# Retention's heads and the last attention of an eight-layer block in another order

## The chip, the core and the metric

The kernel runs on one core of a Trainium2 chip. The metric is the device time of one execution in microseconds. TensorE does the matmuls and transposes, VectorE (DVE), ScalarE (ACT) and GpSimd (POOL) the elementwise work, and SyncE (SP) issues the weight transfers. Each engine works through its own queue in order and waits on semaphores.

## The reference

The input is 256 tokens of width 1024. Eight layers follow each other, all in fp32: stick-breaking attention (16 heads), a squared-ReLU MLP, retention (4 heads, chunks of 128), an MLP, gated linear attention, a convolutional FFN, NSA attention (here the "last attention"), and another FFN. Cut to the two that the change touches:

```python
# retention: q, k (4 heads x 256), v, g (4 heads x 512) = split(h @ w_in); q, k rotated
scores = einsum('bhnid,bhnjd->bhnij', qc, kc) * decay_in      # per 128-token chunk
o = inner + cross                                             # (B, 4, S, 512)
o = (o - mean(o)) * rsqrt(var(o) + eps)                       # per head
y = silu(g) * o;  out = y @ w_out                             # (2048 x 1024)

# NSA attention: 16 query heads in 4 groups over shared keys and values
k_cmp, v_cmp = gelu(blocks(kv) @ w1) @ w2                     # 15 overlapping blocks of 32
p_cmp = masked_softmax(q @ k_cmp * scale); o_cmp = p_cmp @ v_cmp
# with 256 tokens all 4 blocks of 64 are selected and the window of 512 covers all:
o_sel = masked_softmax(rope(q) @ k_sel) @ v_sel               # causal
o_win = masked_softmax(rope(q) @ k_win) @ v_win               # causal
out = (g0 * o_cmp + g1 * o_sel + g2 * o_win) @ w_o
```

## The kernel before

**Weights.** All large weights come as 212 pieces of 128 x 2048 fp32, numbered in the order of use (`ws`). SP streams half pieces into `ring`. ScalarE rounds each half to fp32r (`w_hi`, L1105), VectorE subtracts that for the rest (`w_lo`, L1500), and a product is three fp32r matmuls, hi*hi, hi*lo, lo*hi (`mm3`, L538 to L540). There are four slots for split pieces: `refill(g)` on ScalarE and VectorE splits piece g + 4 once TensorE has finished piece g. Where `refill` stands in an engine's queue is written out by hand. `transposed` makes features x tokens for one piece, `natural` tokens x features for two, `accumulate` and `close` add output pieces into banks 0 to 3.

**Retention.** After query and key pieces, seven pairs of pieces (c = 1 to 7) make values and gates. After pair 3 come the scores of the four heads. A head's output (`ret_out`, L771 and L774) comes after pairs 5, 6, 7 and then once more. `ret_norm` (VectorE) takes its statistics (L1782, L1783) and multiplies by the gate (L1785), GpSimd raises the variance to -0.5 (L416), `ret_scale` (ScalarE) multiplies (L1285). When all four heads are on the way, TensorE runs `keep_clock(3)` (L503), matmuls whose results nobody reads, then turns the eight pairs of 128 columns (`transpose_pair`, L652) between six output pieces G_RET+24 to G_RET+29, and closes with G_RET+30 and G_RET+31.

**The last attention.** Pieces from G_NSA on: two for values, four for compression input and keys (G_NSA+2 to +5), four for queries (+6 to +9), four for the compression's first layer (+10 to +13), four for the output (+14 to +17). Around them on TensorE: the input is turned a second time under another gain (`turn_over("7b", t)`), a small product makes the gates, `ns_swap` multiplies by a permutation for the rotation. VectorE adds positions to the blocks (L1954, 32 instructions), scales, and adds the rope products (L1981, L1988). The keys stand twice in `ns_kd`, each copy with zeros in the other 64 partitions (memset by GpSimd).

Then 16 steps `it`, first the eight pairs of heads of branch 0, then those of branch 1. A step is: `ns_qk_` (L1028, L1029), 128-row products for two heads into banks 4 and 5; `ns_scores` (VectorE): mask added (L2065), maximum (L2070); `ns_exp` (ScalarE, L1439), four exponentials with their sums; `ns_coef` (VectorE): reciprocal times gate (L2078, L2081); a product on GpSimd (L487); `ns_t_`, six transposes (L1036) into banks 6 and 7; `ns_copy` (ScalarE, L1444); `ns_pv_` (L1050, L1051) into banks 0 to 3, where all sixteen heads stay open. Scores run two steps ahead. The compressed branch (`ns_cmp_...`) is fitted in, `keep_clock(4)` stands before the steps and `keep_clock(3)` after them. Only then come the splits of the outputs (L1468, L1554) and the output pieces.

## Time and profile before

| | |
|---|---|
| time, median of 3 runs | 1426.49 us (1425.15 to 1429.76) |
| profiled execution | 1426.23 us, span 1424.5 us |
| busy: TensorE, VectorE, ScalarE, GpSimd | 1366.0, 922.6, 724.5, 122.6 us |
| mean granted TensorE clock | 0.986 |
| weights moved | 231 MB at 162 GB/s |

Times in the profile count from the start of the span. A matmul's record has its pipeline's end in it, so records of neighbours overlap, and the distance of starts is the cost of one. An fp32 matmul is two records. The granted clock is a share of 2.4 GHz; 0.5 would be 1.2 GHz throughout.

### The profile page before, as it was taken

Reading aid. Unit: us, or ns where it says so; the run is one execution under the profiler, and the core shown is the slowest. Engines: PE = TensorE matmul, PEld = TensorE weight load, DVE = VectorE, ACT = ScalarE, POOL = GpSimd, SP = SyncE. Lnnn points to the kernel's source line nnn. Section 1 sums busy time; section 2 is a strip of 40 time slices with the busy share of each in tenths; the row PEclk is TensorE's granted clock in tenths of the full one; section 3 lists DMA queues with packets and bytes.
Section 4 is the critical chain, followed back from the end, with each engine's and each line's share of the span. In section 5 each row is a group of like instructions: output and inputs, shape, how many; then the busy total and the mean of one; then the engine's idle time right before and its main releaser. Section 6 shows DMA issues by size and latency. Waiting matters only on the chain.

```text
span 1424.5 us, 22775 instructions
## 1 busy us (share of the span) xinstructions
PE 1366.0 (96%) x8754; PEld 1218.0 (86%) x8754; DVE 922.6 (65%) x1353; ACT 724.5 (51%) x1139; POOL 122.6 (9%) x123
## 2 busy tenths in 40 slices
PE   8999999999999899999999999999999778999997
PEld 7887999889987679998888789999889556899996
DVE  5666655557645456555577569777768765697775
ACT  5555444445344345444473456555474455565552
POOL 0101000003400000000002300000004133000000
PEclk9999999999999999999999999999999999999999
DMA  6435655555644346555554345555463101355551
GB/s 237 156 124 197 209 182 197 183 173 189 194 161 165 102 150 212 182 198 183 172 163 148 118 150 184 192 185 187 168 221 120 45 31 59 126 191 186 189 192 64
DMA packets 63309, 231.06 MB, mean 162 GB/s; under 512 B 7024, under 2 KB 7280, under 8 KB 63216
## 3 DMA queue, kind: packets, MB, share of 16 engines
q1 hardware_dynamic: 61632, 224.42, 46.9%
q10 hardware_dynamic: 1584, 5.31, 1.1%
q8 instruction: 69, 1.13, 0.3%
q14 instruction: 24, 0.20, 0.0%
HBM read 228.66 MB, written 1.05 MB: 161 GB/s over the span
## 4 chain that ended last, share of the span: by engine, by line
PE 85%; DVE 6%; ACT 3%; DMA 2%; issue 2%; POOL 1%; SPq 0%; POOLq 0%; DVEq 0%; ACTq 0%
PE ps L538 26%; PE ps L540 26%; PE ps L539 26%; DMA ring<-ws 2%; DVE w_lo L1500 2%; ACT w_hi L1105 1%; PE ps L852 1%; POOL arena L487 1%; PE ps L515 1%; PE ps L1029 1%; ACT x_hi L1121 1%; PE ps L1036 1%; DVE arena L2065 0%; PE ps L1028 0%; DVE arena L2070 0%
## 5 line engine op out<-in xcount | busy, mean ns | idle before, releaser
L1500 DVE TENSOR_TENSOR w_lo<-ring,w_hi 128x1024 fp32r<-128x1024 f32 x424 | 514.2, 1253 | 188.6 <-ACT w_hi L1105 188.2
L1105 ACT ACTIVATE w_hi<-ring 128x1024 fp32r<-128x1024 f32 x424 | 429.5, 1054 | 283.6 <-PE ps L540 216.6
L538 PE MATMUL ps<-x_hi,w_hi 128*128 128x256 f32 x1664 | 473.8, 285 | 2.5 <-DVE x_lo L1516 2.5
L539 PE MATMUL ps<-x_lo,w_hi 128*128 128x256 f32 x1664 | 471.8, 284 | 0.0
L540 PE MATMUL ps<-x_hi,w_lo 128*128 128x256 f32 x1664 | 471.7, 283 | 0.0
L538 PEld LDWEIGHTS ps<-x_hi,w_hi 128*128 128x128 f32 x1664 | 320.3, 192 | 5.8 <-issue 4.7
L539 PEld LDWEIGHTS ps<-x_lo,w_hi 128*128 128x128 f32 x1664 | 320.4, 193 | 1.0
L540 PEld LDWEIGHTS ps<-x_hi,w_lo 128*128 128x128 f32 x1664 | 320.2, 192 | 0.0
L538 PE MATMUL ps<-w_hi,y_hi 128*128 128x512 f32 (+1 forms) x624 | 244.2, 391 | 8.4 <-issue 8.0
L539 PE MATMUL ps<-w_lo,y_hi 128*128 128x512 f32 (+1 forms) x624 | 240.4, 385 | 0.0
L540 PE MATMUL ps<-w_hi,y_lo 128*128 128x512 f32 (+1 forms) x624 | 240.0, 385 | 0.0
L538 PEld LDWEIGHTS ps<-w_hi,y_hi 128*128 128x128 f32 x624 | 117.7, 189 | 33.2 <-issue 10.2
L540 PEld LDWEIGHTS ps<-w_hi,y_lo 128*128 128x128 f32 x624 | 117.5, 188 | 23.9
L539 PEld LDWEIGHTS ps<-w_lo,y_hi 128*128 128x128 f32 x624 | 117.8, 189 | 22.3 <-issue 1.0
L538 PE MATMUL ps<-w_hi,x_hi 128*128 128x512 f32 x240 | 97.7, 407 | 4.2 <-DVE w_lo L1500 4.1
L540 PE MATMUL ps<-w_hi,x_lo 128*128 128x512 f32 x240 | 94.5, 394 | 0.0
L539 PE MATMUL ps<-w_lo,x_hi 128*128 128x512 f32 x240 | 94.2, 392 | 0.0
L392 POOL TENSOR_TENSOR stat<-stat,power 128x1 f32<-128x1 f32 x20 | 11.5, 583 | 917.1 <-DVE stat L1493 917.1
L1549 DVE SCALAR_TENSOR_TENSOR arena<-ps,arena 128x512 f32<-128x512 f32 x64 | 44.2, 690 | 70.7 <-PE ps L540 70.7
L1187 ACT ACTIVATE arena<-arena,sm 128x256 f32<-128x256 f32 x88 | 48.2, 596 | 60.2 <-DVE arena L1549 60.2
L1121 ACT ACTIVATE x_hi<-ps,sm 128x128 fp32r<-128x128 f32 x144 | 39.1, 382 | 65.8 <-PE ps L515 65.8
L1155 ACT ACTIVATE arena<-ps 128x512 f32<-128x512 f32 x32 | 19.2, 598 | 92.8 <-PE ps L540 92.8
(205 smaller groups left out, 1238.9 us busy)
## 6 DMA issues: line engine op xcount, KB each, us to landing
ring<-ws SPq DMA_DIRECT2D x424, 512.0 KB, 4.7
tab<-tables ACTq DMA_DIRECT2D x3, 550.0 KB, 4.2
rowg<-rows ACTq DMA_DIRECT2D x3, 512.0 KB, 6.1
h<-x SPq DMA_DIRECT2D x2, 512.0 KB, 4.4
out<-arena SPq DMA_DIRECT2D x2, 512.0 KB, 2.6
arena<-decay ACTq DMA_DIRECT2D x1, 768.0 KB, 9.3
sm<-small ACTq DMA_DIRECT2D x1, 642.0 KB, 5.8
arena<-narrow ACTq DMA_DIRECT2D x1, 296.0 KB, 2.7
```

The source lines that it names most:

```text
L487: r = gp.tensor_tensor(v, v, f, ALU.mult)
L515: r = nc.tensor.transpose(ps[:, 4 + k // 2, t * T + (k % 2) * P:t * T + (k % 2 + 1) * P], h[:, t, k * P:(k + 1) * P], ident)
L538: mm(o, lh, rh, start=start, stop=False, skip_group_check=True)
L539: mm(o, lh, rl, start=False, stop=False, skip_group_check=True)
L540: return mm(o, ll, rh, start=False, stop=stop, skip_group_check=True)
L852: r = mm(o, keys, q, start=True, stop=True, skip_group_check=True)
L1105: A(w_hi[:, g % RING, c:c + HALF], ring[:, q % RAW, :], ACT.Copy).then_inc(hi_ready, 1)
L1121: r = A(x_hi[:, k, t * P:(t + 1) * P], ps[:, 4 + b, t * T + (k % 2) * P:t * T + (k % 2 + 1) * P], ACT.Copy, scale=gain(n, k))
L1155: A(relu[:, u % 2, :], ps[:, bank(u), :], ACT.Relu).then_inc(freed, 1)
L1187: r = A(conv[:, u % 2, e, :], conv_in[:, u % 2, e, :], ACT.Identity, scale=par(u, 4 + e), bias=par(u, 6 + e))
L1500: V.tensor_tensor(w_lo[:, g % RING, v], ring[:, q % RAW, :], w_hi[:, g % RING, v].bitcast(F32), ALU.subtract).then_inc(lo_ready, 1)
L1549: return V.scalar_tensor_tensor(dst, src.rearrange("p (a t) -> p a t", t=T), by, sc.unsqueeze(1).broadcast_to([P, 2, T]), ALU.mult, ALU.mult)
```

## The change

**Retention.** The outputs of heads 0 to 3 are computed inside the gate pairs 4 to 7, in banks given by `rt_o`, and heads 0 and 1 are turned inside pairs 6 and 7, heads 2 and 3 inside output pieces G_RET+25 and G_RET+27 (banks `rt_t`). `ret_norm` moves in front of the refills of its pair. `keep_clock(3)` goes.

**The last attention.** The arena is laid out anew. The second turning stands between pieces G_NSA+4 and +5 and goes to `y_hi`, `y_lo`. The compression's four pieces come after the first query piece, as G_NSA+7 to +10, and the other three query pieces are +11 to +13; the host's order of pieces follows. The steps run by pairs: `it // 2` is the pair of heads, `it % 2` the branch. Steps 0 to 3 lie between the compression pieces and in query piece +11, steps 4 to 6 between the other query pieces; from step 4 on scores are three steps ahead. Scores use 64 rows for each head: each key stands in both halves of the partitions (VectorE writes one half, ScalarE copies the other, `ns_kd_other`), with no zeros. `ns_scores` becomes four `tensor_tensor_reduce`, which add the mask, negate and take the minimum. The copies of turned scores are split: bank 6 by ScalarE, bank 7 by VectorE. A pair's sum over three branches is made in 128 columns of banks 6 and 7 (`ns_o`), then split by `ns_hi` (ScalarE) and `ns_lo` (VectorE) into `x_hi`, `x_lo`; the compressed branch is in two halves (`c`). With banks 0 to 3 free, output pieces G_NSA+14 and +15 are added in eight parts inside the steps (`ns_fill`, six matmuls each); +16 and +17 close as before. The 32 block additions become two instructions on GpSimd, whose rotation products of queries move to steps 3 to 5. Both `keep_clock` go.

The diff, cut to its core and moved left (retention and attention on TensorE, then ScalarE, then VectorE):

```diff
+rt_o = ((0, 1), (2, 3), (0, 1), (6, 7))
+rt_t = ((2, 3), (0, 1), (4, 5), (6, 7))
...
+    pe.wait_ge(*((ret_decayed, 4), (ret_decayed, 4), (ret_o_free, 2), (ret_vg, 14))[hd])
+    pe.wait_ge(ret_vg, 8)
...
+def ret_turn(hd):
+    pe.wait_ge(ret_y, 2 * hd + 2)
+    pe.wait_ge(*((ret_o_free, 4), (ret_o_free, 6), (ret_vg, 16), (ret_o_free, 8))[hd])
+    for j in range(2):
+        transpose_pair(rt_t[hd][j], rt_g, 2 * hd + j).then_inc(ret_transposed, 1)
...
+    then = {4: {(1, 0): lambda: ret_out(0)},
+            5: {(0, 1): lambda: ret_out(1)},
+            6: {(0, 1): lambda: ret_out(2), (1, 0): lambda: ret_turn(0)},
+            7: {(0, 1): lambda: ret_out(3), (1, 0): lambda: ret_turn(1)}}.get(c)
...
-ret_out(3)
-pe.wait_ge(ret_vg, 16)
-keep_clock(3)
...
+pe.wait_ge(ret_yT_lo, 4)
+accumulate(G_RET + 24, (0, 1), True)
+accumulate(G_RET + 25, (2, 3), False, mid=lambda: ret_turn(2))
+accumulate(G_RET + 26, (4, 5), False)
+accumulate(G_RET + 27, (6, 7), False, mid=lambda: ret_turn(3))
+pe.wait_ge(ret_yT_lo, 6)
+accumulate(G_RET + 28, (0, 1), False)
+accumulate(G_RET + 29, (2, 3), False)
+pe.wait_ge(ret_yT_lo, 8)
+close([(G_RET + 30, (4, 5)), (G_RET + 31, (6, 7))], 3)
...
+def ns_qk(it):
+    pr, br = it // 2, it % 2
+    if it < 2:
+        pe.wait_ge(nsa_kd_other, it + 1)
+        pe.wait_ge(nsa_sin, 2)
+    if it >= 5:
+        pe.wait_ge(nsa_cmp_scores_copied, 1 if it < 6 else 2)
+    if it >= 6:
+        pe.wait_ge(nsa_cmp_pT_copied, 1 if it < 8 else 2)
+    pe.wait_ge(nsa_roped, pr // 2 + 1)
+    if it:
+        pe.wait_ge(nsa_max, it)
     for i in range(2):
-        kd, q = ns_kd[i][:, br, pr // 2, :], ns_qr[:, pr, :]
-        mm(ps[:, 4 + i, 0:P], q[:, 0:P], kd[:, 0:P], start=True, stop=True)
-        r = mm(ps[:, 4 + i, P:384], q[:, P:T], kd, start=True, stop=True)
+        v = slice(64 * i, 64 * i + 64)
+        kd, q = ns_kd[v, br, pr // 2, :], ns_qr[v, pr, :]
+        mm(ps[:, 4 + i, 0:P], q[:, 0:P], kd[:, 0:P], start=True, stop=True, skip_group_check=True)
+        r = mm(ps[:, 4 + i, P:384], q[:, P:T], kd, start=False, stop=True, skip_group_check=True)
...
+def ns_t(it):
     pe.wait_ge(nsa_p, it + 1)
+    if it:
+        pe.wait_ge(nsa_pT_copied, it)
+        pe.wait_ge(nsa_pT_copied2, it)
+    if it >= 4:
+        pe.wait_ge(nsa_oT_lo, max(it // 2, 2))
     for i in range(2):
...
+def ns_pv(pr):
+    pe.wait_ge(nsa_pT_copied, max(2 * pr + 2, 4))
+    pe.wait_ge(nsa_pT_copied2, max(2 * pr + 2, 4))
+    pe.wait_ge(nsa_cmp_pT_copied, pr // 4 + 1)
+    if pr:
+        pe.wait_ge(nsa_oT_lo, pr)
+    for t in range(TT):
+        mm(ns_o[:, t, :], ns_vbd[:, pr // 4, 2 * (pr % 4):2 * (pr % 4) + 2, :], ns_cp[:, 2 * (pr // 4) + t, :],
+           start=True, stop=False, skip_group_check=True)
+    for br in range(2):
+        for i in range(2):
+            v = ns_v[:, :, br * 256 + (pr // 2) * 64:br * 256 + (pr // 2) * 64 + 64]
+            p_ = ns_p[(2 * pr + br) % 4][:, i, :]
+            for t in range(TT):
+                o = ps[64 * i:64 * i + 64, 6 + t, 384:512]
+                r = mm(o, v[:, 0, :], p_[:, t * P:(t + 1) * P], start=False, stop=False, skip_group_check=True)
+            r = mm(o, v[:, 1, :], p_[:, T:384], start=False, stop=br == 1, skip_group_check=True)
...
+def ns_fill():
+    n = filled[0]
+    filled[0] += 1
+    i, k, t = n // 4, n // 2 % 2, n % 2
+    if n == 0:
+        pe.wait_ge(nsa_roped, 4)
+    if t == 0:
+        pe.wait_ge(nsa_oT_lo, n // 2 + 1)
+        split(G_NSA + 14 + i, k)
+    r = add(G_NSA + 14 + i, (2 * i, 2 * i + 1), t, k, i == 0, False, (x_hi, x_lo))
...
+ns_qk(0)
+ns_first(0, 1)
+ns_qk(1)
+ns_first(1, 0)
+ns_t(0)
+ns_qk(2)
+ns_first(1, 1)
+ns_t(1)
+ns_qk(3)
 ns_hidden_t()
-keep_clock(4)
-for it in range(16):
-keep_clock(3)
...
+pe.wait_ge(nsa_gate_in, 1)
+transposed(G_NSA + 11, 1, src=mixed, mid=lambda: ns_t(2))
+ns_t(3)
+ns_swap(3)
+transposed(G_NSA + 12, 0, src=mixed, mid=lambda: (ns_cmp_kv(), ns_qk(4)))
+ns_cmp_qk(0)
+ns_qk(5)
+ns_swap(4)
+pe.wait_ge(nsa_roped, 2)
+transposed(G_NSA + 13, 1, src=mixed, mid=lambda: ns_cmp_t(0))
+ns_pv(0)
+ns_cmp_qk(1)
+ns_swap(5)
+ns_qk(6)
+ns_pv(1)
+for it in range(4, 16):
+    ns_t(it)
+    if it == 5:
+        ns_cmp_t(1)
+        ns_fill()
+    if it + 3 < 16:
+        ns_qk(it + 3)
+    if it in (6, 7, 10, 11, 14):
+        ns_fill()
+    if it % 2:
+        ns_pv(it // 2)
+        if it in (9, 13):
+            ns_fill()
+pe.wait_ge(nsa_oT_lo, 8)
+close([(G_NSA + 16, (4, 5)), (G_NSA + 17, (6, 7))], 8, src=(x_hi, x_lo))
...
+    if c >= 5:
+        ret_scale(c - 5)
     refill(G_RET + 9 + 2 * c)
-    if c >= 6:
-        ret_scale(c - 6)
-ret_scale(2)
+refill(G_RET + 24)
+ret_turned(2)
+refill(G_RET + 25)
 ret_scale(3)
-for g in range(10):
-    if g < 8:
...
+refill(G_RET + 26)
+refill(G_RET + 27)
+ret_turned(3)
+refill(G_RET + 28)
+refill(G_RET + 29)
...
+ns_exp(1)
+refill(G_NSA + 9)
+ns_copy(0)
+ns_exp(2)
+refill(G_NSA + 10)
+ns_inner_(1)
+ns_copy(1)
+ns_exp(3)
 ns_gelu_square()
-for it in range(16):
-    if it:
...
+ns_copy(2)
+ns_gelu_tanh()
+refill(G_NSA + 11)
+ns_copy(3)
+ns_cmp_keys()
+ns_exp(4)
+refill(G_NSA + 12)
+ns_cmp_exp(0)
+ns_exp(5)
+ns_cmp_copy(0)
+refill(G_NSA + 13)
+ns_hi(0)
+ns_cmp_exp(1)
+ns_hi(1)
+for it in range(4, 16):
+    ns_copy(it)
     if it == 5:
-        act.wait_ge(nsa_cmp_shifted, 1)
-        A(ns_cs[:, :, :, :], ns_cs[:, :, :, :], ACT.Exp).then_inc(nsa_cmp_exp, 1)
...
+        ns_cmp_copy(1)
+    if it + 2 < 16:
+        ns_exp(it + 2)
+    if it in (10, 15):
+        refill(G_NSA + (14 if it == 10 else 15))
+    if it % 2:
+        ns_hi(it // 2)
...
 def ns_scores(it):
     dve.wait_ge(nsa_scores, it + 1)
     if it >= 3:
         dve.wait_ge(nsa_pT, it - 2)
-    s = ns_s[:, it % 3, :, :]
-    V.tensor_tensor(s, ps[:, 4:6, 0:384],
-                    tab[:, C_CAUSAL:C_CAUSAL + 384].unsqueeze(1).broadcast_to([P, 2, 384]), ALU.add)\
-     .then_inc(nsa_masked, 1)
-    dve.wait_ge(nsa_masked, it + 1)
-    for t in range(2):
-        r = V.tensor_reduce(ns_m[:, it % 2, :, t], s[:, :, P * t:P * t + P * (t + 1)], AX.X, ALU.max,
-                            negate=True)
+    if it >= 2:
+        dve.wait_ge(nsa_exp, it - 1)
+    for i in range(2):
+        for t in range(TT):
+            v = slice(P * t, P * t + P * (t + 1))
+            r = V.tensor_tensor_reduce(ns_s[it % 3][:, i, v], ps[:, 4 + i, v],
+                                       tab[:, C_CAUSAL + v.start:C_CAUSAL + v.stop], -1.0, 3.0e38,
+                                       ALU.add, ALU.min, ns_m[:, it % 2, i, t:t + 1])
     r.then_inc(nsa_max, 1)
...
 ns_scores(0)
+V.memset(ns_kc[:, :, :], 0.0)
 ns_coef(0)
 ns_scores(1)
+refill(G_NSA + 8)
+ns_coef(1)
+ns_copy(0)
+ns_scores(2)
+refill(G_NSA + 9)
+ns_coef(2)
+link(V.memset(ns_h[:, 2:4, :, :], 0.0))
+ns_copy(1)
+ns_scores(3)
 ns_gelu_inner()
-for it in range(16):
+ns_coef(3)
+refill(G_NSA + 10)
+ns_copy(2)
+ns_queries(1)
+ns_gelu()
+ns_copy(3)
+ns_rope(1)
+refill(G_NSA + 11)
+ns_cmp_values()
+ns_scores(4)
+ns_queries(2)
+ns_cmp_scores(0)
+ns_coef(4)
+ns_scores(5)
+ns_cmp_p(0)
+ns_rope(2)
+ns_coef(5)
+refill(G_NSA + 12)
+ns_queries(3)
+ns_lo(0)
+ns_cmp_scores(1)
+ns_rope(3)
+ns_scores(6)
+refill(G_NSA + 13)
+ns_lo(1)
+for it in range(4, 16):
+    ns_copy(it)
+    if it + 3 < 16:
+        ns_scores(it + 3)
+    if it == 4:
+        ns_cmp_p(1)
     if it + 2 < 16:
-        ns_scores(it + 2)
-    if it == 3:
...
+        ns_coef(it + 2)
+    if it % 2:
+        ns_lo(it // 2)
+    if it == 11:
+        refill(G_NSA + 14)
+refill(G_NSA + 15)
```

## Rows read from the trace of the kernel before

**Rows 1.** Page, part 1: engine, busy us, share of the span, instructions.
```profile
PE 1366.0 (96%) x8754; PEld 1218.0 (86%) x8754; DVE 922.6 (65%) x1353; ACT 724.5 (51%) x1139; POOL 122.6 (9%) x123
```

**Rows 2.** Waits of TensorE, 380 to 500 us: total, times, longest.
```profile
PE ps L538 <- issue: 5.6, 1, 5.6
```

**Rows 3.** Waits of TensorE, 1050 to 1220 us.
```profile
PE ps L1036 <- POOL arena L487: 7.1, 7, 2.5
PE ps L1028 <- DVE arena L1988: 6.0, 1, 6.0
```

**Rows 4.** Windows: length, busy us and instructions per engine, granted clock, DMA.
```profile
465.35:480.01 14.66, 9.03 (x30) 4.47 (x30) 9.45 (x18) 8.35 (x13) 1.39 (x2) 0.88 0.31 110
480.01:487.28 7.27, 7.27 (x26) 5.83 (x27) 1.09 (x2) 0.15 (x1) 0.00 (x0) 0.77 0.01 2
1039.67:1063.00 23.33, 23.27 (x195) 23.07 (x193) 13.71 (x14) 15.57 (x21) 0.00 (x0) 1.00 0.74 254
1063.00:1118.77 55.77, 46.77 (x342) 42.37 (x343) 47.67 (x88) 23.66 (x37) 16.03 (x8) 0.93 0.35 120
1118.77:1203.40 84.63, 69.08 (x435) 50.25 (x435) 54.90 (x114) 50.19 (x161) 31.97 (x32) 0.94 0.12 38
1203.40:1214.30 10.90, 10.90 (x48) 9.04 (x49) 2.36 (x2) 2.01 (x2) 0.00 (x0) 1.00 0.14 37
```

**Rows 5.** Chain, 430 to 500 us: start, us, engine and line.
```profile
438.37 1.72 PE ps L771 x4
440.09 0.86 PE ps L774 x2
...
487.28 0.44 PE ps L652 x4
```

**Rows 6.** Timeline of TensorE in stick-breaking attention, from 43 us.
```profile
43.10 0.50 PE L670 MATMUL ps<-arena 64*128 64x128 f32 x4
43.42 0.61 PE L672 MATMUL ps<-arena 64*128 64x256 f32 x4
43.96 0.38 PE L538 MATMUL ps<-x_hi,w_hi 128*128 128x256 f32 x1
```

**Rows 7.** Timeline of TensorE in the last attention, from 1151 us.
```profile
1150.81 0.87 PE L1036 MATMUL ps<-sm,arena 128*128 128x128 f32 x6
1151.52 0.39 PE L1028 MATMUL ps<-arena 128*128 128x128 f32 x2
...
1152.17 0.38 PE L1028 MATMUL ps<-arena 128*128 128x128 f32 x2
```

**Rows 8.** Groups by form, 1118 to 1203 us: count, busy, mean ns, idle before.
```profile
L1439 ACT ACTIVATE arena<-arena 128x256 f32<-128x256 f32 x32 | 15.9, 496 | 0.0
L2065 DVE TENSOR_TENSOR arena<-ps,tab 128x768 f32<-128x768 f32 x16 | 15.3, 954 | 14.8 <-PE ps L1029 14.8
...
L1439 ACT ACTIVATE arena<-arena 128x128 f32<-128x128 f32 x32 | 12.5, 392 | 6.5 <-DVE arena L2070 6.5
...
L1439 ACT ACTIVATION_READ_ACCUMULATOR arena<-arena 128x1 f32 x64 | 12.1, 190 | 0.0
...
L2070 DVE TENSOR_REDUCE arena<-arena 128x2 f32<-128x512 f32 x16 | 10.8, 676 | 0.0
...
L2070 DVE TENSOR_REDUCE arena<-arena 128x2 f32<-128x256 f32 x16 | 6.7, 420 | 0.6
L503 PE MATMUL ps<-sm 128*128 128x512 f32 x14 | 6.5, 607 | 0.0
```

**Rows 9.** Groups of VectorE, whole span.
```profile
L1712 DVE TENSOR_TENSOR_SCAN arena<-arena,tab 128x384 f32<-128x384 f32 x16 | 14.6, 956 | 17.7 <-ACT arena L1232 17.7
```

**Rows 10.** Timeline of GpSimd, 1163 to 1171 us.
```profile
1164.72 3.50 POOL L487 TENSOR_TENSOR arena<-arena 128x256 f32<-128x256 f32 x2 [3.85 <-DVE arena L2081]
1169.60 1.61 POOL L487 TENSOR_TENSOR arena<-arena 128x256 f32<-128x256 f32 x2 [1.38 <-DVE arena L2081]
```

**Rows 11.** Windows of 10 us.
```profile
1180.00:1190.00 10.00, 7.84 (x62) 6.07 (x59) 9.09 (x17) 5.71 (x21) 5.12 (x4) 1.00 0.41 133
```

More of the change, by code:

```diff
@@ new lines, in ns_swap, with ns_first @@
+                b, src = (4 + i, ns_k[:, i, :, :]) if i < 2 else (i % 2, ns_q[:, 2 * (i - 2):2 * (i - 2) + 2, :])
+                mm(ps[:, b, :], swap, src, start=True, stop=True).then_inc(nsa_swapped, 1)
+            def ns_first(i, e):
+                g = G_NSA + 7 + 2 * i + e
+                s = g % RING
+                pe.wait_ge(nsa_blocks, i + 1)
+                for l in range(8):
+                    if l % 4 == 0:
+                        split(g, l // 4)
+                    w, x = l * 256, (16 * i + 8 * e + l) * 60
+                    r = mm3(ps[:, 2 + i, 0:256], ns_xhf[:, x:x + P], ns_xlf[:, x:x + P],
+                            w_hi[:, s, w:w + 256], w_lo[:, s, w:w + 256], e + l == 0, e * l == 7)
+                r.then_inc(done, 1)
@@ new lines, in ns_kd_other @@
+            def ns_kd_other(br):
+                act.wait_ge(nsa_kd, br + 1)
+                for o in range(2):
+                    r = A(ns_kd[64 - 64 * o:128 - 64 * o, br, o:o + 3:2, :], ns_kd[64 * o:64 * o + 64, br, o:o + 3:2, :],
+                          ACT.Copy)
+                r.then_inc(nsa_kd_other, 1)
+            refill(G_NSA + 2)
+            ns_raw_(0)
+            refill(G_NSA + 3)
+            ns_raw_(1)
+            tiles("7b", 0, y_hi, 0)
+            refill(G_NSA + 4)
+            tiles("7b", 1, y_hi, 0)
@@ new lines, in _ @@
+            refill(G_NSA + 5)
+            for i in range(2):
+                act.wait_ge(nsa_blocks_f32, i + 1)
+                A(ns_xh[:, i, :, :], ns_x[:, i, :, :], ACT.Copy).then_inc(nsa_blocks_hi, 1)
+            for br in range(2):
+                ns_kd_other(br)
+            refill(G_NSA + 6)
+            act.wait_ge(nsa_gate_scaled, 1)
+            A(ns_gt[0:48, :], ns_gt[0:48, :], ACT.Sigmoid).then_inc(nsa_gates_transposed, 1)
+            refill(G_NSA + 7)
+            act.wait_ge(nsa_gates_turned, 1)
@@ L1960, in _, with ns_queries @@
[L1960 to L1966 removed]
+            def ns_queries(u):
+                dve.wait_ge(done, G_NSA + (7 if u == 0 else 11 + u))
+                scaled(ns_q[:, 2 * u:2 * u + 2, :], ps[:, u % 2, :], scale, 0.125).then_inc(nsa_q_in, 1)
@@ new lines, in _ @@
+            ns_unit(0)
+            refill(G_NSA + 2)
+            ns_unit(1)
+            refill(G_NSA + 3)
+            tiles("7b", 0, (y_hi, y_lo), 0)
+            ns_unit(2)
+            refill(G_NSA + 4)
+            tiles("7b", 1, (y_hi, y_lo), 0)
+            ns_unit(3)
+            refill(G_NSA + 5)
+            for i in range(2):
+                dve.wait_ge(nsa_blocks_hi, i + 1)
+                V.tensor_tensor(ns_xl[:, i, :, :], ns_x[:, i, :, :], ns_xh[:, i, :, :].bitcast(F32), ALU.subtract)\
+                 .then_inc(nsa_blocks, 1)
@@ new lines, in _ @@
+            for br in range(2):
+                ns_sin(br)
+                dve.wait_ge(nsa_sin, br + 1)
+                dve.wait_ge(nsa_cos_product, br + 1)
+                for o in range(2):
+                    v = slice(64 * o, 64 * o + 64)
+                    r = V.tensor_tensor(ns_kd[v, br, o:o + 3:2, :], ns_t1[v, br, :, :], ns_t2[br][v, :, :], ALU.add)
+                r.then_inc(nsa_kd, 1)
+            ns_queries(0)
+            refill(G_NSA + 6)
+            dve.wait_ge(nsa_small_proj, 1)
```

557 lines of the change are left out of this document (218 added, 339 removed).

## The prediction

> **What bounds the kernel now.** I read the busy shares first: TensorE holds 96% of the span [rows 1], so a change pays where it removes TensorE idle time, dead work, or half-clock time, and nowhere else. Then the waits of TensorE around the two stages that the diff touches. In retention there is one wait, 5.6 us [rows 2]. In the last attention (NSA) there are many; the largest sums are for GpSimd's coefficient product (L487) and the rope sums of VectorE (L1988) [rows 3]. The windows say how much there is in all and at which clock [rows 4]. Then the chain, for what one instruction group costs on TensorE [rows 5], and the groups by form for the queues behind it [rows 8].
>
> **Retention.** From the end of the last gate piece (465.35) to the first output piece (480.01) pass 14.66 us [rows 4]. Of these, work that stays: ret_out of heads 2 and 3, each 1.72 + 0.86 = 2.58, so 5.16, and three pairs of transposes at 0.44 = 1.32 [rows 5]. The other 8.2 us are keep_clock and the wait, and both go. The wait is a chain over other engines: ret_norm on VectorE, the power on GpSimd, ret_scale on ScalarE, then the copies of the turned pairs. Then the first output piece runs at a low clock: 7.27 us, granted clock 0.77, that is a stretch at 1.2 GHz (the lower of the two levels) after the 5.6 us wait; a piece at full clock takes 10.90 / 2 = 5.45 [rows 4]. Another 1.8. Sum: 10.0.
>
> Is something late in its place? I followed each new wait. A gate pair is now 10.9 + 2.58 (+ 0.88 for two turned pairs), 13.5 to 14.4 us. ret_norm(hd) stands ahead of the refill in VectorE's queue; it takes about 3.2 us (four operations of 512 elements at 0.68 as the reduction of that size [rows 8], three small ones) from the gate's evacuation, and the refill behind it fills a slot four pieces (some 22 us) ahead, so TensorE doesn't see that. ret_turn(0) asks for a head normalised a whole pair earlier. The tightest is ret_turn(1): it needs ret_norm(2) off banks 0 and 1, which stands behind refill(G_RET+21); I find it done about 1.4 us early. ret_turned(2) on ScalarE waits for the piece that used its y tile (done of G_RET+25) with refill(25) behind it: again 20 us of cover. If one of these misses, it costs 1 to 2 us: the stage gives 8 to 10.3.
>
> **NSA, what goes.** I take the stage from 1039.67 (its third piece) to 1214.30, where the last two output pieces start: 174.6 us. In it TensorE is idle 55.77 - 46.77 = 9.0 and 84.63 - 69.08 = 15.55, so 24.55 [rows 4]. keep_clock takes 6.5 [rows 8]. The scores of a step cost 2 x 0.65 = 1.3 us with full 128-row keys, half of them zeros (1151.52 to 1152.17 is one head) [rows 7]; the new form, 64 rows for each of two heads, is in stick-breaking attention: 43.10 to 43.96 = 0.86, since the two heads overlap [rows 6]. 16 x 0.43 = 6.9 saved. Stretches at 1.2 GHz inside the two windows (clock 0.93 and 0.94) [rows 4] cost about 4 beyond the idle time: my estimate, as idle time is in that mean too. Transposes, pieces and swaps keep their columns. Floor: 174.6 - 24.55 - 6.5 - 6.9 - 4 = 132.6 us.
>
> **NSA, what the new order waits for.** The chain of a step is: scores, mask and maximum on VectorE, four exponentials on ScalarE (2 x 0.39 + 2 x 0.50 = 1.8), coefficient on VectorE (two operations of four elements, 0.4 with the hand-over), product on GpSimd (1.61 for its two instructions alone, 3.50 where VectorE's weight refill runs beside it [rows 10]), transposes 0.87 [rows 7]. Three steps of lead on TensorE are 10 us, more than this chain. So GpSimd, 7.1 us of waits before, drops out; what is left is queues in order.
>
> The new instruction, a fused tensor_tensor_reduce, isn't in this trace. Before, a step has 0.95 + 0.42 + 0.68 = 2.05 on VectorE [rows 8]. Now four instructions of 128, 256, 128, 256 elements. Low end: the rate of those rows (256 elements in 0.42, 512 in 0.68: 0.16 fixed and 1 ns an element), so 0.29 and 0.42, 1.4 a step. High end: the scan, 384 elements in 0.956, so 2.07 ns an element [rows 9]: with it 2.2, and with four reads of the accumulator at ScalarE's 0.19 for such a read [rows 8], up to 3.0. I take 1.8: the full rate, since its nearest row is the mask addition (PSUM plus table), and 0.1 for each minimum written out. The page "VectorE: DVE Perf Modes" of the Trainium skill (Two Vector instructions with no wait between them) says that an op that also writes its accumulator is two instructions; that speaks against the fusion, eight entries where there were three. ScalarE's rows of that kind agree, VectorE has none here.
>
> The thirty-two block additions leave VectorE for two instructions of 960 elements on GpSimd: 2.0 each by the 768 elements in 1.61, 4.4 by the 3.50 [rows 10]. Both are due only at the first compression piece, some 20 us after their inputs; cover enough, cost nothing. If it were gone: up to 4. The page "SBUF — State Buffer" of the Trainium skill (Who interferes with whom) has this as a lock: a VectorE op with two SBUF inputs and a GpSimd op that reads SBUF exclude one another. The two rows of GpSimd agree (1.61 and 3.50); it would give the same sum, only place the stretched copies beside the refills.
>
> Walked in order with these prices, TensorE waits at:
> 1. gates and first rope (VectorE has the keys, q scaling, a refill and the gate product before them): 1.3.
> 2. ns_hidden_t: ScalarE has the exponentials of step 2 (1.8), a refill (2.0 [rows 4]) and ns_inner_(1) (0.4) to do, 4.2; TensorE has at that time 0.7 of compression and scores 3 (0.86): 2.6.
> 3. ns_t(3), for VectorE's copy behind refill(G_NSA+10), and cmp_qk(0): 1.2.
> 4. ns_t(4), which wants the low half of pair 1. On VectorE stand before it, from the last swap on, the last rope (1.5), scores 6 (1.8), refill(G_NSA+13) (2.4 [rows 4]) and ns_lo(1) (0.4), 6.7 with hand-overs; TensorE has scores 6 and value product 1, 3.1: 3.6.
> 5. ns_cmp_t(1): in the first loop turn VectorE does scores 7 (1.8, once they are there) and the compressed probabilities (1.6: two operations of 256 elements, three small); TensorE has ns_t(5), 0.87: 2.7.
> 6. Each pair's end: transposes of the next pair share banks 6 and 7 with the sums, so they wait for ns_hi and ns_lo (256 elements each, 0.4 and a hand-over each), 1.0; covered by ns_fill only after steps 9 and 13. With the refill in step 11 and the last pair: 9.0 in all.
>
> Sum 20.4, I take 21. The waits 2, 4 and 5 are long enough to bring the clock down, as the long ones before did [rows 4], and there is no keep_clock now: three times 1.5 to 2, so 5. NSA: 174.6 - 132.6 - 21 - 5 = 16 less. The output pieces G_NSA+14 and 15 are inside the loop as ns_fill (8 x 6 matmuls of 512 columns, 10.9 us); they are in both sums. Weights: no DMA is added, SP's queue keeps its length and streams pieces four ahead; the compression pieces only change places with three query pieces. What is moved to ScalarE (four key copies of half the partitions, eight ns_hi in place of four copies) is in the walk.
>
> **Sum.** The profiled execution took 1426.2 (span 1424.5), the median of the runs is 1426.5. 10 + 16 = 26 less: **1400** us. By the bounds: some twelve of the sixteen steps are on the path. With 1.4 for the fused step (12 x 0.4) and no clock loss the stage gives 10 more: 1390. With 2.7 a step 12 x 0.9 = 11 come back: 1411.
>
> **Rivals.**
> - *The waits almost vanish.* VectorE is busy 47.7 + 54.9 us of 140.4 [rows 4] and the order leaves it other work at each wait. For: stick-breaking attention and GLA interleave likewise. Against: six waits above each have a named instruction in front. If 8 of the 26 us (waits and clock) remain: 1426 - 10 - 34 = 1382 to 1390.
> - *VectorE becomes the bound.* The fused instruction runs at the scan's rate or its reads are dear (2.7 to 3.0 us a step). For: two operations and a sum in one. Against: the mask addition, its nearest row, runs at 1 ns an element. 12 steps x 0.9 to 1.2, so 11 to 14 back: 1411 to 1414.
> - *Nothing in NSA.* The fills and query pieces only move work, and every gap is closed by a new one of its size: 1416.
> - *Slower: the half clock.* keep_clock stood where TensorE's work was thin. If the steps of the loop stay at 1.2 GHz after the wait at ns_t(4), the loop's TensorE work of 42 us takes as much again (12 transposes 10.4, 9 scores 7.7, fills 10.9, and 6 value products of fourteen 128-column matmuls: 0.215 each by the 512 columns in 0.86 [rows 5], twelve of them overlapping by a third as the scores do, 2.15): 26 gained, 42 less the 12 of waits in the loop lost, so 1430. It decides from 26 us of uncovered half-clock work on. For: [rows 4] show 0.93 and 0.94 over both halves. Against: from 1180 on TensorE is busy only 7.84 of 10 us, in short waits, and the clock stays at 1.00 [rows 11].
>
> **Chances.** Forecast (1392 to 1408) 0.57; waits vanish 0.18; VectorE the bound 0.16; nothing in NSA 0.05; slower 0.04. The range takes in the first two and most of the third: 1386 to 1412. This kernel's runs can tell 0.3%, 4 us. Faster 0.95, same 0.01, slower 0.04.
>
> **What the profile after would show.** Retention: no TensorE wait over 1 us between the gates and the close, clock 1.00 there, no L503-like matmuls in it; else the first part is wrong. NSA: the fused instruction at 0.27 to 0.42 us for 128 and 256 elements with a short read behind; scores of a step 0.86 on TensorE; no wait on GpSimd's product; waits at ns_hidden_t, ns_t(4), ns_cmp_t(1), and about 1 us before the transposes of even steps. The prediction falls if the fused form costs over 0.7 us for 256 elements, or if the low clock lasts beyond each of the long waits.

## The result, and the profile after

The changed kernel takes 1393.1 us (median of 4 runs, 1391.5 to 1396.5) beside 1427.4 us for the kernel before, run with it: ratio 0.976, 95% interval 0.974 to 0.978. That is 34 us less; 26 were forecast, with a range of 1386 to 1412. The profiled execution took 1391.5 us (span 1389.8). It is the fastest of the four, and the one with the highest mean granted clock: 0.995, where the others have 0.992, 0.990 and 0.989 in the order of their times.

The page's busy shares, which answer to [rows 1]:

```profile
PE 1343.2 (97%) x8814; PEld 1204.1 (87%) x8814; DVE 909.6 (65%) x1423; ACT 722.0 (52%) x1149; POOL 122.1 (9%) x123
```

TensorE was the bound and still is. It did 23 us less of work in more instructions, and its share rose by one point. VectorE has 70 more instructions and 13 us less work.

Windows of the kernel after (length, busy us and instructions per engine, granted clock, DMA share, GB/s): first retention, from the scores to the turn of the second row tile; then the last attention (NSA), from its third piece to the close of the last two output pieces; then three parts of it: up to the transposes of step 4, the 12 us from there, and the whole loop from there. They answer to [rows 4].

```profile
408.51:512.03 103.52, 103.52 (x461) 82.31 (x460) 55.84 (x72) 46.28 (x57) 6.43 (x4) 1.00 0.48 163
1028.40:1179.55 151.15, 133.70 (x1086) 115.78 (x1084) 105.82 (x288) 90.66 (x232) 43.78 (x40) 0.99 0.34 112
1063.00:1125.00 62.00, 53.85 (x442) 47.21 (x442) 50.56 (x132) 36.67 (x88) 18.49 (x16) 1.00 0.37 121
1125.00:1137.00 12.00, 9.14 (x64) 6.53 (x64) 5.72 (x28) 5.12 (x20) 3.22 (x4) 0.86 0.23 80
1125.00:1178.61 53.61, 45.24 (x362) 34.92 (x362) 25.94 (x116) 29.11 (x102) 16.10 (x20) 0.97 0.12 39
```

The first row is retention without a gap: TensorE is busy for all of 103.52 us at clock 1.00. Between the same two instructions the kernel before took 113.59 (411.35 to 524.94), so 10.1 less. The second row is NSA: 151.15 against 174.63, so 23.5 less. Of the 151.15 us TensorE is busy for 133.70 and idle for 17.45 (before: 150.02 and 24.6). By distances of starts the 23.5 us are 7.1 of waits, 6.4 of keep_clock and some 11 of scores (25.6 to 14.7, low clock in both); everything else together costs about 1 us more than before. The only low clock of the stage is in the 12 us of the fourth row, 0.86. The remaining difference of the two profiled executions lies in code that is the same in both: 2.8 us less ahead of retention and 1.6 more between the stages. Both are differences between executions, not between the kernels. The first: in the second run of the changed kernel (below) retention ends 1.8 us later than in this profile, without any edit. The second is one stretch at the lower clock that begins at 799.7, behind a wait of 2.3 us: of the fourteen profiles of this case eight have it and take 516.0 us between the stages, the other six, the kernel before among them, 514.3 to 514.4, with the same waits.

The waits of TensorE in NSA (total us, times, longest), which answer to [rows 3]:

```profile
PE ps L1027 <- DVE x_lo L2158: 5.5, 4, 2.4
PE ps L959 <- ACT arena L1450: 2.1, 1, 2.1
PE ps L994 <- DVE arena L2126: 2.0, 1, 2.0
PE ps L1039 <- ACT arena L1492: 1.6, 2, 0.9
PE ps L939 <- DVE arena L1639: 1.4, 1, 1.4
PE ps L1027 <- DVE arena L2166: 1.1, 1, 1.1
PE ps L544 <- DVE x_lo L2158: 0.9, 1, 0.9
PE ps L1078 <- ACT arena L1521: 0.9, 1, 0.9
...
PE ps L1014 <- DVE arena L2064: 0.6, 1, 0.6
...
PE ps L1027 <- POOL arena L491: 0.2, 1, 0.2
```

The first row is step transposes (L1027) waiting for the low half of a pair (L2158): once 2.4 before step 4, then three times 1.02, before steps 6, 8 and 12. GpSimd's product, 7.1 us in [rows 3], is down to 0.2, and the 6.0 for the rope sums to 0.6 (L2064). No single wait is longer than 2.4.

Groups of VectorE's instructions in the steps, 1080 to 1186 us, by form:

```profile
L2138 DVE CUSTOM_DVE_ANT_0 arena<-ps,tab 128x256 f32<-128x256 f32 x28 | 11.7, 419 | 0.0
...
L2138 DVE CUSTOM_DVE_ANT_0 arena<-ps,tab 128x128 f32<-128x128 f32 x28 | 8.0, 287 | 5.2 <-PE ps L1015 5.1
...
L2138 DVE DVE_READ_ACCUMULATOR2_ANT arena<- 128x1 f32 x56 | 4.6, 83 | 0.0
```

These are the two sizes of the fused instruction and its read, the price that the trace of before could not give. The timeline of VectorE below, up to the longest wait, shows them in line:

```profile
1121.06 0.28 DVE L2138 CUSTOM_DVE_ANT_0 arena<-ps,tab 128x128 f32<-128x128 f32 x1
1121.27 0.08 DVE L2138 DVE_READ_ACCUMULATOR2_ANT arena<- 128x1 f32 x1
1121.27 0.42 DVE L2138 CUSTOM_DVE_ANT_0 arena<-ps,tab 128x256 f32<-128x256 f32 x1
...
1122.16 2.35 DVE L1590 TENSOR_TENSOR w_lo<-ring,w_hi 128x1024 fp32r<-128x1024 f32 x2
1124.44 0.42 DVE L2158 TENSOR_TENSOR x_lo<-ps,x_hi 128x256 fp32r<-128x256 f32 x1
1125.89 0.56 DVE L2166 COPY arena<-ps 128x384 f32<-128x384 f32 x1 [1.03 <-PE ps L1027]
```

A read starts at the same time as the next fused instruction and so costs nothing; a step of four takes 1.19 us (1121.06 to 1122.24). Behind it stands the weight refill, 2.35 us, and only then the low half, at whose end (1124.86) TensorE's transposes start (1125.00).

### The profile page after: what moved, and what is told of

It is laid out like the page before. It is cut to its first block, busy times and chain, and to the rows that moved or that the text cites. A ratio compares the mean times of both kernels' runs of the same rounds, so it can differ in the third digit from the quotient of the medians.

```text
span 1389.8 us, 23087 instructions
## 1 busy us (share of the span) xinstructions
PE 1343.2 (97%) x8814; PEld 1204.1 (87%) x8814; DVE 909.6 (65%) x1423; ACT 722.0 (52%) x1149; POOL 122.1 (9%) x123
## 4 chain that ended last, share of the span: by engine, by line
PE 87%; DVE 5%; ACT 3%; DMA 2%; issue 2%; POOL 1%; SPq 0%; POOLq 0%; DVEq 0%; ACTq 0%
PE ps L544 26%; PE ps L546 26%; PE ps L545 26%; DMA ring<-ws 2%; DVE w_lo L1590 2%; ACT w_hi L1148 1%; PE ps L854 1%; PE ps L521 1%; ACT x_hi L1164 1%; PE ps L1047 1%; PE ps L1027 1%; PE ps L777 0%; DVE arena L2138 0%; ACT arena L1141 0%; PE ps L1015 0%
## 5 line engine op out<-in xcount | busy, mean ns | idle before, releaser
L544 PE MATMUL ps<-x_hi,w_hi 128*128 128x256 f32 x1600 | 454.5, 284 | 2.5 <-DVE x_lo L1606 2.5
L545 PE MATMUL ps<-x_lo,w_hi 128*128 128x256 f32 x1600 | 452.7, 283 | 0.0
L546 PE MATMUL ps<-x_hi,w_lo 128*128 128x256 f32 x1600 | 452.7, 283 | 0.0
L544 PE MATMUL ps<-w_hi,y_hi 128*128 128x512 f32 x560 | 220.3, 393 | 2.3 <-issue 2.3
L545 PE MATMUL ps<-w_lo,y_hi 128*128 128x512 f32 x560 | 219.0, 391 | 0.0
L546 PE MATMUL ps<-w_hi,y_lo 128*128 128x512 f32 x560 | 218.7, 391 | 0.0
L544 PE MATMUL ps<-w_hi,x_hi 128*128 128x512 f32 (+1 forms) x304 | 121.9, 401 | 5.8 <-DVE w_lo L1590 4.8
L546 PE MATMUL ps<-w_hi,x_lo 128*128 128x512 f32 (+1 forms) x304 | 116.3, 382 | 0.0
L545 PE MATMUL ps<-w_lo,x_hi 128*128 128x512 f32 (+1 forms) x304 | 115.9, 381 | 0.0
L544 PEld LDWEIGHTS ps<-w_hi,x_hi 128*128 128x128 f32 x304 | 57.4, 189 | 21.9 <-DVE w_lo L1590 5.5
```

Of the source, the lines that this page charges most:

```text
L544: mm(o, lh, rh, start=start, stop=False, skip_group_check=True)
L545: mm(o, lh, rl, start=False, stop=False, skip_group_check=True)
L546: return mm(o, ll, rh, start=False, stop=stop, skip_group_check=True)
```

## Experiments

The experiments were run in four groups on three chips: the second run of the changed kernel (1394.4 us) stands beside the late refill, the moved parts and both; retention alone, the fused instruction, the 128-row scores and the shorter lead form the second group; the blocks, the output parts and the clock the third; the last kernel the fourth. In each group the kernel before was run too, with medians of 1427.4, 1426.5, 1428.3 and 1427.1 us, so two groups compare within 1 to 2 us. "More" and "less" below are against the changed kernel's 1393.1 and 1394.4, and a ratio is always against the kernel before of the same group. "The stretch" is that from the first rope swap of NSA (L939) to the start of the close, read from each kernel's timeline of TensorE: 123.4 us in the profile after, 124.3 in that second run of the same kernel.

**The changed kernel again.** No edit.

> The changed kernel once more, on the chip and beside the runs of the next three kernels. Both theories expect 1393.1 us within 1 us; it gives the mark for differences of 2 to 5 us.

Measured: 1394.4 us (1393.8 to 1395.0, 5 runs), ratio 0.977 (0.975 to 0.979). A difference of 1 us between two groups of runs means nothing here. Its profile has nearly the same waits as the profile after, but two stretches at the lower clock in NSA instead of one.

**Retention alone.** The kernel before, with only the part of the diff that concerns retention (rt_o and rt_t, ret_out and ret_turn inside the gate pieces, the new order on ScalarE and VectorE).

> The kernel before with the retention part of the change alone. Theory: the 10.0 us of that part are on TensorE's path and independent of the last attention: 1427.4 - 10.0 = 1417.4, ratio 0.993. Rival: the gain is given back in the stages behind (weights or queues that come late there): within 2 us of the kernel before.

Measured: 1416.6 us (1415.0 to 1418.4), before beside it 1426.5; ratio 0.993 (0.991 to 0.995), 9.9 us less. From scores to the second turn pass 103.7 us (410.31 to 513.99), with no wait of TensorE from 380 to 500. The theory holds and nothing is given back behind it; so some 24 of the 34 us are NSA's.

**The fused instruction taken apart.** ScalarE's exponentials then take the scores with their own sign (scale=-1.0 goes).

```diff
-                for i in range(2):
-                    for t in range(TT):
-                        v = slice(P * t, P * t + P * (t + 1))
-                        r = V.tensor_tensor_reduce(ns_s[it % 3][:, i, v], ps[:, 4 + i, v], ...)
+                V.tensor_tensor(s, ps[:, 4:6, 0:384], <causal table>, ALU.add).then_inc(nsa_masked, 1)
+                dve.wait_ge(nsa_masked, it + 1)
+                for t in range(2):
+                    r = V.tensor_reduce(ns_m[:, it % 2, :, t], s[:, :, P * t:P * t + P * (t + 1)], AX.X, ALU.max,
+                                        negate=True)
```

> The changed kernel with the fused instruction taken apart again, as it was before: a mask addition for both heads, then two negated maxima (2.05 us a step by the rows of before, where the fused form takes 1.19). Theory of the prediction: some twelve of the sixteen steps lie on the path, 12 x 0.86 = 10 us more, 1403. Rival: three steps of lead cover VectorE (busy only half of the loop), so that just the places where its queue is already late lose: 0 to 3 us more, 1393 to 1396.

Measured: 1403.1 us (1401.5 to 1404.2), ratio 0.983 (0.982 to 0.985): 9 to 10 more. The size is that of "twelve steps on the path", but the trace doesn't show twelve delayed steps. Its waits and one window (TensorE):

```profile
PE ps L1027 <- DVE x_lo L2160: 6.3, 4, 3.2
PE ps L959 <- ACT arena L1450: 2.8, 1, 2.8
...
PE ps L1014 <- DVE arena L2141: 1.8, 2, 1.4
PE ps L1039 <- issue: 1.7, 1, 1.7
PE ps L1027 <- POOL arena L491: 1.3, 1, 1.3
```
```profile
1129.83:1142.00 12.17, 10.03 (x52) 7.17 (x54) 5.87 (x14) 4.86 (x19) 1.61 (x2) 0.60 0.24 79
```

The stretch is 131.3 us, 7 to 8 more. About 5 of them are waits, grown in five places by 0.7 to 1.1 each; the rest is the clock, which after the 3.19 us wait stays near its lower level (1.2 GHz) for most of 12 us (0.60 granted, where the same place in the kernel after has 0.86). So VectorE's time counts where its queue is already late, and the longest wait is paid a second time in the clock.

**Scores over all 128 rows.**

```diff
-                    kd, q = ns_kd[v, br, pr // 2, :], ns_qr[v, pr, :]
+                    kd, q = ns_kd[:, br, pr // 2, :], ns_qr[:, pr, :]
```

> The changed kernel with scores over all 128 rows for each head, so 1.3 us a step instead of 0.86 on TensorE; the scores are then sums over both heads of a pair, which leaves the result wrong and the amount of all other work as it is. Theory: TensorE bounds the stage, 16 x 0.43 = 6.9 us, less what lies in its waits: 5 to 7 more, 1398 to 1400. Rival: the other engines' chains set the pace, the longer scores fill waits: 0 to 2 more.

Measured: 1399.8 us (1397.7 to 1400.1), ratio 0.981 (0.979 to 0.983): 5 to 7 more, as the theory has it. The profiled execution (the fastest of the four) shows less: its stretch is 126.7, 2.4 to 3.3 more. There the longer scores filled waits (that for the hidden units, L959, fell from 2.1 to 0.3). What the other runs lost beyond that was not profiled, so between 2 and 7 us is what can be said for the row tiles.

**Scores two steps ahead.** In the loop, on TensorE, ScalarE and VectorE (ns_scores and ns_coef, moved like the lines below); GpSimd's order needs no edit. In step 5 the scores also come ahead of ns_cmp_t(1).

```diff
-                if it + 3 < 16:
-                    ns_qk(it + 3)
+                if 5 <= it < 14:
+                    ns_qk(it + 2)
...
-                if it + 2 < 16:
-                    ns_exp(it + 2)
+                if 5 <= it < 15:
+                    ns_exp(it + 1)
```

> The changed kernel with scores two steps ahead instead of three in the loop (steps 5 to 15), on all four engines. Theory: the third step of lead is what took GpSimd's product off the path; with two the chain of 5.8 to 7.7 us stands against 5.6 to 7.4 us of TensorE work, and waits of up to 2 us ended by the product (L491) come back in nine steps: 3 to 10 us more, 1396 to 1403. Rival: pairs and fills alone do it, the lead is slack: 0 to 1 more.

Measured: 1410.5 us (1409.3 to 1413.2), ratio 0.989 (0.987 to 0.991): 16 to 17 more, beyond the theory's 10. Waits:

```profile
PE ps L1027 <- POOL arena L491: 14.9, 6, 4.0
PE ps L1027 <- DVE x_lo L2158: 5.5, 4, 2.4
```

The named wait is the right one, but it comes in five steps, not nine, and is not "up to 2 us": it stands before the transposes of every odd step from 7 on, 2.0 at steps 7 and 11 and 3.0 to 4.0 at 9, 13 and 15 (and 0.4 before step 3). The product itself takes its 1.61 us in both kernels; it starts later, since the coefficient (and all before it) starts later. The loop's clock is 0.91 from 1138 to the end, where the kernel after has 1.00 (1137 to 1178.6). Of all parts of the change that were undone here, this one is worth most.

**The block additions back on VectorE.**

```diff
+                for l in range(16):
+                    o = ns_x[:, i, l, :].rearrange("p (a n) -> p a n", n=15)
+                    ...
+                    r = V.tensor_scalar(o, ns_raw[:, i, :, 2 * l:2 * l + 16 * 14 + 1:16], pe_, None, ALU.add)
```

> The changed kernel with the additions of the compression blocks back on VectorE, thirty-two instructions of 60 elements at 345 ns with their hand-over (6.7 us busy in the kernel before), and the two on GpSimd left out. Theory: VectorE's queue is what gates, rope and query pieces wait for there, so that 2 to 5 of these microseconds show, 1395 to 1398. Rival: the fold into the lead of the query piece covers them all: within 1 us of the changed kernel.

Measured: 1401.9 us (1401.6 to 1403.7), ratio 0.982 (0.981 to 0.984): 7.5 to 9 more, outside both. A wait and a window:

```profile
PE ps L932 <- DVE arena L1632: 7.8, 1, 7.8
```
```profile
1058.00:1074.00 16.00, 8.35 (x60) 7.18 (x59) 15.84 (x43) 3.87 (x5) 3.24 (x1) 0.82 0.22 76
```

The third rope swap (L932) waits 7.8 us for the scaled query (L1632), where the changed kernel waits 1.4 (0.7 in its second profile): VectorE is busy for 15.84 of 16.00 us, with the 32 additions (7.0 us) in front of the keys' rope and the query. Before the change four query pieces lay between the additions and the work that reads them; now the first swap of the queries comes right behind its piece. GpSimd does the same work in two instructions of 2.34 us each, and nothing waits for them. The part's worth is not the engine time saved but the place in the queue.

**The output parts out of the loop.** All eight ns_fill after it, with both refills of those slots.

> The changed kernel with the two output pieces (eight parts, 10.9 us of TensorE work) taken out of the loop and done after it, all else equal. Theory: the loop's chains, not TensorE's work, end its waits only at pair ends; by the waits that the parts stand beside, 1 to 4 us open up: 1394 to 1397. Rival one: the parts were wholly in idle time, all 10.9 us show: 1404. Rival two: they covered nothing: 1393.

Measured: 1399.5 us (1398.6 to 1402.4), ratio 0.981 (0.980 to 0.983): 5 to 6 more, between the theory's 1 to 4 and the rival's 10.9. The loop from the transposes of step 4 to the last value product (windows):

```profile
1128.48:1176.49 48.01, 36.03 (x315) 27.68 (x315) 23.76 (x114) 25.20 (x98) 16.09 (x20) 0.93 0.07 22
```

48.0 us without the parts, 53.6 with them (above): of 10.9 us of work 5.6 cost time in the loop, and 5.3 lie in waits or in what the lower clock takes (0.93 here, 0.97 above). Those 5.3 are what the parts inside the loop save, and the 5 to 6 more measured agree.

**A late refill, parts moved, and both.**

```diff
             ns_scores(6)
-            refill(G_NSA + 13)
             ns_lo(1)
             for it in range(4, 16):
                 ns_copy(it)
+                if it == 5:
+                    refill(G_NSA + 13)
```
```diff
                 if it == 5:
-                    ns_cmp_t(1)
                     ns_fill()
+                    ns_cmp_t(1)
...
-                if it in (6, 7, 10, 11, 14):
+                if it in (6, 10, 14):
                     ns_fill()
                 if it % 2:
                     ns_pv(it // 2)
-                    if it in (9, 13):
+                    if it in (7, 9, 11, 13):
                         ns_fill()
```

> VectorE's weight refill of piece G_NSA+13 goes from before the low half of pair 1 to after the copy of step 5. Theory: the wait before the transposes of step 4 (2.39 us, ended by that low half) is the refill's 2.4 us and goes; the stretch at the lower clock right behind it goes as well: 2.4 to 4.1 us less than the changed kernel, 1389.0 to 1390.7. Rival: another queue is as late there (ScalarE's copy of the high half), or the refill only moves the delay to the low half of pair 2: within 0.7 us of the changed kernel.

> The pieces of output work inside the loop change places: in step 5 ahead of the turned compressed probabilities, in steps 7 and 11 behind the value product instead of ahead. Theory: they then lie over the waits before those turns (2.0 us) and before the transposes of steps 8 and 12 (1.02 us each): 1.4 + 1.0 + 1.0 = 3.4 us less, 1389.7. Rival: where they stood they covered waits of the same size (the value products wait for ScalarE's copies), which open now: within 0.7 us of the changed kernel.

> The two edits before this one together. Theory: the waits are apart and their gains add: 5.8 to 7.5 us less than the changed kernel, 1385.6 to 1387.3. Rival: both shorten one chain, so that together they give no more than the larger alone: 1389 to 1391.

Measured: the refill 1391.6 us (1388.7 to 1393.3), ratio 0.974 (0.972 to 0.977), 2.8 less than the changed kernel beside it; the parts 1391.9 (1387.9 to 1395.8), ratio 0.974 (0.972 to 0.977), 2.5 less, but with runs on both sides; both 1389.8 (1387.6 to 1391.4), ratio 0.974 (0.971 to 0.976), 4.7 less. VectorE and TensorE with the late refill:

```profile
1125.44 0.08 DVE L2138 DVE_READ_ACCUMULATOR2_ANT arena<- 128x1 f32 x1
1126.34 0.42 DVE L2158 TENSOR_TENSOR x_lo<-ps,x_hi 128x256 fp32r<-128x256 f32 x1 [0.82 <-ACT x_hi L1496]
```
```profile
1126.91:1139.00 12.09, 9.09 (x78) 6.78 (x78) 9.46 (x31) 5.75 (x22) 4.21 (x4) 1.00 0.25 82
```

The low half now waits for ScalarE's high half instead of the refill, TensorE's wait is 1.02 instead of 2.39, and the clock behind it is 1.00 instead of 0.86. The stretch is 121.5 (late refill) and 119.4 (both), 2 to 3 and 4 to 5 less. With the parts moved the waits before steps 8 and 12 and before the turned probabilities are gone, and one of 0.63 before a value product has come; from step 4 to the close pass 53.3 us (1130.57 to 1183.87) instead of 54.6. But that profiled run is the slowest of its five: it lost the gain again ahead of step 4, where the clock was 0.92 in a stretch that the edit doesn't touch. The late refill gives as much as its theory says (2.4 to 4.1 less), though the wait shrinks only by 1.4, as ScalarE's half comes next. For the parts the runs overlap those of the changed kernel, so the time alone shows nothing. Both together give 4.7 less, about the sum of the two (5.3) but not the 5.8 to 7.5 of the theory; 1389.8 lies in the range of the rival, whose mechanism (no more than the larger alone, 2.8) it doesn't bear out.

**The clock kept up.** Three matmuls of no use in front of the wait before step 4.

> The changed kernel with three matmuls of no use (keep_clock, bank 2) in front of the wait before the transposes of step 4. Theory: it is that idle 2.39 us that brings the granted clock from 1.00 to 0.86 in the 12 us behind it; with the engine busy the clock stays at 1.00 there, about 1.7 us less, 1391 to 1392. Rival: the matmuls, 3 x 0.43 to 0.61 us, are no shorter than what they save, or the clock falls all the same: 1393 to 1395.

Measured: 1393.7 us (1392.2 to 1394.6), ratio 0.976 (0.975 to 0.978): no difference. Windows before and behind the place:

```profile
1087.00:1125.50 38.50, 37.86 (x290) 33.52 (x291) 29.11 (x75) 15.05 (x42) 12.40 (x9) 0.93 0.27 91
1125.50:1137.50 12.00, 9.33 (x69) 6.30 (x67) 6.94 (x30) 5.12 (x20) 3.05 (x4) 1.00 0.25 87
```

Behind it the clock is 1.00, as the theory says, but a stretch at the lower level lies ahead of it in this execution (0.93). TensorE hardly waits in that window, but the window starts right behind a wait, the one for the hidden units, and the low clock begins inside that wait:

```profile
1086.35 0.47 PE L959 MATMUL ps<-sm,arena 60*128 60x60 f32 x2 [2.31 <-ACT arena L1451]
```
```profile
1085.80:1092.70 6.90, 6.35 (x30) 6.25 (x31) 4.17 (x10) 2.94 (x13) 2.77 (x3) 0.51 0.30 102
1092.70:1125.50 32.80, 32.16 (x264) 27.82 (x263) 25.25 (x67) 13.32 (x33) 9.66 (x8) 1.00 0.28 95
```

The repetition of the changed kernel has such a stretch too, from 0.2 us behind the same wait on (0.96 over 1089 to 1128); the profile after has the wait (2.1) and no low clock. The kernel with the blocks on VectorE has the same two waits (2.39 and 1.98 us) without filler and a clock of 1.00 behind them. So such a wait is not enough to bring the clock down, and the filler not enough to gain anything.

**All named waits covered.** The two edits together, a part of output work behind each of the pairs 2 to 7, and ns_inner_(1) ahead of refill(G_NSA+10) on ScalarE, whose refill(G_NSA+15) goes behind the loop.

> The changed kernel with every wait whose releaser the runs so far named put under cover: the late refill and the part ahead of the turned probabilities as before, a part of output work behind each of the pairs 2 to 7 (the transposes or the close behind them waited 0.93 to 1.02 us each), and ScalarE's copy of the hidden units (L1450, wait 0.7 to 2.1 us) ahead of its refill of G_NSA+10. Theory: these waits are independent; 4.6 us as with the two edits together, 0.7 to 2.1 for the copy, 1.0 for pair 2 and 0.9 for the close: 7 to 9 us less than the changed kernel's 1393 to 1394, so 1385 to 1387. Rival: with ends of pairs covered, the value products' waits for ScalarE and the transposes' wait for VectorE's copy (1.1) grow by as much: no better than the two edits together, 1389 to 1390.

Measured: 1391.1 us (1389.5 to 1392.6), ratio 0.975 (0.973 to 0.976): no better than the two edits together (the intervals overlap), as the rival says, though what grew is in the main another wait than the ones it names. The window around the transposes of step 3:

```profile
1087.00:1124.00 37.00, 34.16 (x261) 30.28 (x262) 26.84 (x73) 17.80 (x47) 14.01 (x11) 0.91 0.36 117
```

The waits before steps 6, 8 and 12 and before the close are gone, and so is the one for the hidden units. But before the transposes of step 3 TensorE now waits 2.3 us for GpSimd's product (0.25 before), and the clock of that window is 0.91. TensorE came there 2 us sooner and step 3's chain did not. The wait for the hidden units had covered that chain and was no loss of its own.

## Why the prediction was right, and what it had wrong

Forecast were 1400 us and measured 1393.1, inside the range and 7 below the forecast: the last attention (NSA) gave 23.5 us where 16 were taken.

**Retention: right in mechanism and size.** 10.0 forecast, 10.1 in the trace, 9.9 for this part alone. The lateness that I had looked for (ret_turn(1), ret_turned(2)) shows in no wait.

**NSA, what goes: right.** The floor was 132.6 us, with the low clock that there is (0.86 of 12 us, 1.7) 134.3; TensorE is busy for 133.7. That it fits within 0.6 is in part balance. The 1.3 us for a step's scores is one head doubled; up to the work behind them the trace of before has 1.40 (1151.52 to 1152.92):

```profile
1152.39 0.60 PE L1029 MATMUL ps<-arena 128*128 128x256 f32 x2
1152.92 0.66 PE L1050 MATMUL ps<-arena 128*64 128x256 f32 x4
```

The changed kernel with 128-row scores has 1.12 where an output part follows (1142.30 to 1143.42); 64 rows take 0.86. So the 6.9 could be 4 to 9.

**NSA, the waits: right in place, too long by 3.6 us.** They sum to 17.4 where 21 were taken. By number: 1, gates and first rope, 2.9 (1.3 forecast; the third swap's wait for the query, 1.4, was missing); 2, hidden units, 2.1 (2.6); 3, 0.8 (1.2); 4, step 4, 2.4 (3.6); 5, turned probabilities, 2.0 (2.7); 6, pairs' ends and the rest of the loop, 7.3 (9.0). Five of the six are shorter by a fifth to a third. For 4 and 5 the term behind it is the fused step: 1.8 us taken, 1.19 measured, so 0.6 of the 1.2 and 0.6 of the 0.7 by which they came out shorter. Instead of my 0.29 and 0.42 with 0.1 added for each minimum, they take 0.287 and 0.419 with nothing added, and start 0.07 before the last one ends. Even the low bound, 1.4, was above it. The high end, with 0.19 for each read as on ScalarE, is not what ScalarE's own reads cost, and the trace of before had this: the four exponentials of a step start at 1152.42, 1152.81, 1153.30 and 1153.68, their own length apart, so that the reads lie beside them too. Wait 2 has no fused step in my walk and none in the profile after, where ScalarE stands 0.4 for the weights of its refill (0.6 in the second profile), a term that the walk lacks. The pairs' ends I walked at 1.0 a hand-over, which is what they take (1.02); the four that no part covers make 4.0, and the remaining 5.0 that I had added for the refill in step 11 and the rest of the loop are 3.3. The page "VectorE: DVE Perf Modes" of the Trainium skill (Two Vector instructions with no wait between them) says that such an operation is two instructions. The trace agrees (56 reads of 83 ns for 56 of them) and shows what the second costs here: nothing, as the read lies beside the next instruction.

**The clock: the term furthest off.** I took 5 us for three low stretches, one behind each long wait. The profile after has one (it begins behind the turned compressed probabilities, at 1130.8, and lasts some 3 us; a part's six matmuls take 2.02 us instead of 1.66 there, and the scores behind them 1.59 instead of 0.86), 1.7 us. The second profile of the changed kernel has two, 3.4 us. So the term was too large by 3.3 us in the one and 1.6 in the other, and part of it is the luck of the execution.

Waits (3.6), clock (3.3) and floor (0.6) make the 7.5 us by which the profiled NSA came out faster than forecast. For the fused step it is shown: taken apart, it lengthens wait 4 by 0.8 and wait 2 by 0.5 to 0.7 (ScalarE's exponentials then stand 0.8 for VectorE), and the clock over the 12 us from step 4 on is 0.60 instead of 0.86. For the clock it is not shown. With a shorter wait before step 4 (1.02, the late refill) it stays up there, but so it does in the kernel with the blocks on VectorE, where both waits are as long as in the kernel after. That kernel and wait 2 of the profile after (2.1, clock 1.00 behind it) refute that each long wait costs 1.5 to 2 of clock.

**The rivals.** VectorE did not become the bound (26 of 54 us busy in the loop); its price per element is that of the mask addition. The waits did not almost vanish (of the forecast's 26 us 17.4 remain as waits and 1.7 as clock, where this rival had 8 in all). No gap was replaced by one of its size, and the clock is 0.97 in the loop.

**What I had treated as free.** The move of the block additions is right as forecast (2.34 us each, hidden), but undoing it costs 8 us: without it the rest of the change would have lost a third of NSA's gain. Likewise the third step of lead, which carries 16 us. The parts undone one by one are worth 9 to 10, 2 to 7, 16, 8 and 5 to 6 us, together far more than NSA's 23.5. So they don't add. That each covers waits which the absence of another opens would explain it, but no run undoes two at once. The copies split between ScalarE and VectorE, the order by pairs and the end of keep_clock were not undone by themselves.

**Open.** What the other runs of the kernel with 128-row scores lost beyond its profiled one. And which waits are followed by low clock: in all fourteen profiles each low stretch between the kernel's first matmuls and its last begins inside a wait of TensorE or at most 1.6 us behind one, but the same wait has one in some executions and none in others.

## What to carry to other kernels

When stages are interleaved, walk each engine's queue up to the instruction that TensorE waits for and ask what stands in it that is not due yet: here a refill of 2.4 us was one wait, and 32 small additions would have been another of 7.8. Here the third step of lead was worth more than any single instruction, and without it a wait of 2 to 4 us came in every odd step from 7 on. A wait that is uncovered only by the next chain, as that for the hidden units, moves when it is covered; look at what TensorE reaches next before filling it.
